# Up projection by products over both halves of the activations, high weights first, in a decoder block in fp32r parts

## What is computed

```python
up = rmsnorm(h, g_ffn[layer]) @ w_up[layer]            # 2048 -> 2 * 5632
up = causal_depthwise_conv(up, conv_w[layer], conv_b[layer])
gate, val = jnp.split(up, 2, axis=-1)
h = h + (jax.nn.silu(gate) * val) @ w_down[layer]      # 5632 -> 2048
```

## Time and profile before

| | us |
|---|---|
| median of 3 runs | 2804.72 (2804.52 to 2804.82) |
| the profiled execution | 2804.28 |
| its span, first to last instruction | 2802.8 |
| PE busy | 2797.0 (100%) |
| VectorE (DVE) busy | 2086.1 (74%) |
| ScalarE (ACT) busy | 1248.7 (45%) |

### The profile page before, as it was taken

The page is one execution under the profiler, slowest core; times in us unless marked ns, Lnnn a source line. Parts: engine busy times, 40 slices in busy tenths (PEclk is TensorE's granted clock), DMA queues, the critical chain, the costliest instruction groups (busy, mean ns, idle before and its releaser), DMA issues.

```text
span 2802.8 us, 45334 instructions
## 1 busy us (share of the span) xinstructions
PE 2797.0 (100%) x16930; PEld 2511.9 (90%) x16930; DVE 2086.1 (74%) x3913; ACT 1248.7 (45%) x1701; POOL 428.0 (15%) x579
## 2 busy tenths in 40 slices
PE   9999999999999999999999999999999999999999
PEld 7888888888889998888899999999999999999998
DVE  7776777677778777444468987888788878887884
ACT  5444343443434334333355544444444444544543
POOL 1022144323400000000000111111011101110112
PEclk9999999999999999999999999999999999999999
DMA  5464585666535555444455666666656656666667
GB/s 182 140 177 103 170 204 123 179 190 119 121 111 162 174 167 176 148 134 148 139 175 140 145 137 136 134 138 136 136 136 136 136 136 135 137 137 138 135 136 166
DMA packets 187463, 411.24 MB, mean 147 GB/s; under 512 B 22288, under 2 KB 50320, under 8 KB 186128
## 3 DMA queue, kind: packets, MB, share of 16 engines
q1 hardware_dynamic: 120240, 283.90, 33.2%
q0 software_dynamic: 67040, 124.82, 24.3%
HBM read 347.81 MB, written 112.72 MB: 164 GB/s over the span
## 4 chain that ended last, share of the span: by engine, by line
PE 97%; DVE 2%; ACT 0%; issue 0%; DMA 0%; SPq 0%; DVEq 0%; ACTq 0%
PE bank L1890 12%; PE bank L1892 12%; PE bank L1891 12%; PE bank L2160 11%; PE bank L2162 11%; PE bank L2161 11%; PE bank L2195 6%; PE bank L2196 6%; PE bank L2197 6%; PE bank L2116 3%; PE bank L2117 3%; PE bank L2118 3%; PE bank L1964 1%; PE bank L1998 1%; PE bank L2009 0%
## 5 line engine op out<-in xcount | busy, mean ns | idle before, releaser
L2160 PE MATMUL bank<-v_hi,w_hi 128*128 128x256 f32 x2464 | 697.6, 283 | 0.0
L2162 PE MATMUL bank<-v_hi,w_lo 128*128 128x256 f32 x2464 | 697.3, 283 | 0.0
L2161 PE MATMUL bank<-v_lo,w_hi 128*128 128x256 f32 x2464 | 697.3, 283 | 0.0
L937 ACT ACTIVATE w_hi<-w_raw 128x896 fp32r<-128x896 f32 (+1 forms) x528 | 445.1, 846 | 557.8 <-DVE w_raw L1686 384.5
L1693 DVE TENSOR_TENSOR w_lo<-w_raw,w_hi 128x896 fp32r<-128x896 f32 (+1 forms) x528 | 500.1, 952 | 127.0 <-ACT w_hi L937 125.9
L2160 PEld LDWEIGHTS bank<-v_hi,w_hi 128*128 128x128 f32 x2464 | 472.9, 192 | 2.0 <-issue 0.2
L2161 PEld LDWEIGHTS bank<-v_lo,w_hi 128*128 128x128 f32 x2464 | 472.9, 192 | 1.9 <-issue 0.2
L2162 PEld LDWEIGHTS bank<-v_hi,w_lo 128*128 128x128 f32 x2464 | 472.9, 192 | 0.0
L1890 PE MATMUL bank<-u_hi,w_hi 128*128 128x512 f32 x1000 | 395.4, 395 | 0.2 <-DVE w_lo L1078 0.2
L1892 PE MATMUL bank<-u_hi,w_lo 128*128 128x512 f32 x1000 | 389.9, 390 | 0.0
L1891 PE MATMUL bank<-u_lo,w_hi 128*128 128x512 f32 x1000 | 389.3, 389 | 0.0
(11 more groups left out here) (290 smaller groups left out, 4843.9 us busy)
## 6 DMA issues: line engine op xcount, KB each, us to landing
w_raw<-wslots SPq DMA_DIRECT2D x504, 256.0 KB, 2.7
w_raw<-wstream SPq DMA_DIRECT2D x189, 512.0 KB, 3.6
out_t<-stage POOLq DMA_DIRECT2D x168, 256.0 KB, 4.3
sums_scratch<-wfirst POOLq DMA_DIRECT2D x72, 448.0 KB, 5.6
g_raw<-sums_scratch SPq DMA_DIRECT2D x48, 448.0 KB, 3.3
g_raw<-wgates SPq DMA_DIRECT2D x48, 256.0 KB, 3.0
w_raw<-sums_scratch SPq DMA_DIRECT2D x24, 448.0 KB, 3.4
sums_scratch<-sums_scratch POOLq DMA_DIRECT2D x72, 128.0 KB, 4.7
```

What stands on the lines that cost most here:

```text
L937: act.activation(w4_hi[ring][:, 0:width], w4_raw[ring][:, 0:width], ACT.Copy).then_inc(w4_hi_ready, 1)
L2160: nc.tensor.matmul(out, wh, xh, start=kp == 0 and half == 0, stop=False, skip_group_check=True)
L2161: nc.tensor.matmul(out, wh, xl_, start=False, stop=False, skip_group_check=True)
L2162: ins = nc.tensor.matmul(out, wl, xh, start=False, stop=kp == KP - 1, skip_group_check=True)
```

## The change

From tile 8 on (`WIDE` = 7, 37 tiles) an up product is two matmuls in place of three. The high weights are multiplied with the high and the low activations in one matmul of 512 columns, whose moving operand is a view of two runs of 256 in `v_parts`; the low weights are multiplied with the high activations in one of 256 columns, added to the first half of the same bank. Each of the seven products has a bank of its own (0 to 6), and the two halves of a bank are added when the tile is done. In a slot the seven high matmuls come first, then, after a wait for the low weights, the seven low ones; in the tile's last slot the first three products (`EARLY`) are finished ahead of the other four. ScalarE copies the second halves of the first three banks, then of the other four (`low_halves`), and VectorE adds the first halves to them (`add_halves`), puts the sums together (`combine_wide`) and forms gate and value from them (`take_up_wide`).

The down slots of these tiles go to banks 7, 0, 1 and 7, which each wait for what was in them. A down slot's eight matmuls with high weights come ahead of its four with low weights. `take_down` moves to the head of ScalarE's position right behind the down slot; the fourth down tile's goes to position 2 of the next tile. Three semaphores of the gate stage are merged with later ones, and three new ones come in. The diff, cut to its core:

```diff
+WIDE = 7
+WIDE_PRODUCTS = [(A11, B11), (S2, T2), (S3, T3), (A22, T4), (S1, T1), (A12, B21), (S4, B22)]
+EARLY = 3
 ...
-    v_hi = [sb(f"v_hi{j}", VC, a, F32R) for j, a in enumerate(kp_at)]
-    v_lo = [sb(f"v_lo{j}", VC, a + 4 * VC, F32R) for j, a in enumerate(kp_at)]
+    v_parts = [sb(f"v_parts{j}", 2 * VC, a, F32R) for j, a in enumerate(kp_at)]
+    v_hi, v_lo = [t[:, 0:VC] for t in v_parts], [t[:, VC:2 * VC] for t in v_parts]
 ...
+    early_sum, late_sum = sb("early_sum", 4 * HALF, 28 * K), sb("late_sum", 4 * HALF, tile[10] + 64)
 ...
-    bank = [nc.alloc_psum_tensor(f"bank{j}", [P, SEQ], F32) for j in range(8)]
+    banks = nc.alloc_psum_tensor("bank", [P, 8 * SEQ], F32)
+    bank = [banks[:, j * SEQ:(j + 1) * SEQ] for j in range(8)]
 ...
+    def down_bank(d):
+        if d >= END:
+            return bank[2 + d % GROUP]
+        return bank[(7, 0, 1, 7)[d % GROUP] if wide(d // GROUP + 2) else GROUP + d % GROUP]
 ...
+            def low_halves(f, late):
+                if late:
+                    act.wait_ge(slot_done, START_F[f] + KP)
+                    act.wait_ge(s_raw_ready, f)
+                    act.activation(part_list(late_sum, 4), bank_halves(EARLY, 7, 1),
+                                   ACT.Copy).then_inc(low_copied, 1)
+                else:
+                    act.wait_ge(early_done, f - WIDE + 1)
+                    act.wait_ge(up_out, f - 1)
+                    act.activation(part_list(early_sum, EARLY), bank_halves(0, EARLY, 1),
+                                   ACT.Copy).then_inc(low_copied, 1)
 ...
-                hi_slot(n + 3)
                 f = max(g for g in range(FT) if START_F[g] <= at_)
                 q = at_ - START_F[f]
                 slots_done = place(n)[0]
+                if wide(f) and q == KP:
+                    low_halves(f, False)
+                if f >= WIDE - 1 and f < FT - 1 and q > KP:
+                    take_down(n, GROUP * (f - 2) + q - KP - 1, slots_done)
+                if n not in hi_made:
+                    hi_slot(n + 3)
 ...
-                if f > 2 and q in (2, 4):
+                if 2 < f < WIDE and q in (2, 4):
                     take_down(n, d0 - 2 + (q == 4), slots_done)
+                if f >= WIDE and q == 2:
+                    take_down(n, d0 - 1, slots_done)
 ...
-                        p1_copy(n, f)
-                    if q == KP + 1:
-                        take_down(n, d0, slots_done)
+                        if wide(f):
+                            low_halves(f, True)
+                        else:
+                            p1_copy(n, f)
                     if q == KP + 2:
                         conv_term(n, f, 0)
-                        take_down(n, d0 + 1, slots_done)
                     if q == KP + 3:
                         conv_term(n, f, 1)
                 if f == FT - 1:
                     if q == KP:
-                        p1_copy(n, f)
+                        low_halves(f, True)
+                        hi_slot(n + 4)
+                        hi_made.add(n + 1)
 ...
+            def add_halves(f, late):
+                k = 2 * (f - WIDE) + late
+                sums, j0, j1 = (late_sum, EARLY, 7) if late else (early_sum, 0, EARLY)
+                dve.wait_ge(low_copied, k + 1)
+                dve.tensor_tensor(part_list(sums, j1 - j0), bank_halves(j0, j1, 0), part_list(sums, j1 - j0),
+                                  ALU.add).then_inc(drained, 1)
+            def combine_wide(f):
+                k, done = 2 * (f - WIDE), f * DVE_STEPS4
+                dve.wait_ge(drained, k + 1)
+                dve.tensor_tensor(part(early_sum, 1), part(early_sum, 1), part(early_sum, 0),
+                                  ALU.subtract).then_inc(dve4_step, 1)
+                dve.wait_ge(dve4_step, done + 1)
+                dve.tensor_tensor(part(early_sum, 2), part(early_sum, 1), part(early_sum, 2),
+                                  ALU.subtract).then_inc(dve4_step, 1)
+                dve.wait_ge(drained, k + 2)
+                dve.scalar_tensor_tensor(out=part(early_sum, 3), in0=part(late_sum, 1), scalar=-1.0,
+                                         in1=part(early_sum, 1), op0=ALU.mult, op1=ALU.subtract).then_inc(dve4_step, 1)
+            def take_up_wide(f):
+                done = f * DVE_STEPS4
+                dve.wait_ge(dve4_step, done + 2)
+                dve.tensor_tensor(a_pad[1][:, PAD:PAD + SEQ].rearrange("p (a c) -> p a c", a=2),
+                                  part(early_sum, 2).unsqueeze(1).broadcast_to((P, 2, HALF)),
+                                  part_list(late_sum, 2), ALU.add).then_inc(dve4_step, 1)
+                dve.wait_ge(dve4_step, done + 3)
+                first_last = early_sum[:, :].rearrange("p (b c) -> p b c", c=HALF)[:, 0:4:3, :]
+                dve.tensor_tensor(a_pad[0][:, PAD:PAD + SEQ].rearrange("p (a c) -> p a c", a=2),
+                                  late_sum[:, 2 * HALF:4 * HALF].rearrange("p (a c) -> p a c", a=2),
+                                  first_last, ALU.add).then_inc(up_out, 1)
             def combine(n, f):
+                if wide(f):
+                    add_halves(f, True)
+                    combine_wide(f)
+                    return
 ...
+                if wide(f) and q == KP:
+                    add_halves(f, False)
+                sums(n + 3)
+                lo_slot(n + 2)
 ...
+            def bank_free(f, j):
+                d = GROUP * (f - 3)
+                if f == WIDE:
+                    if j >= GROUP:
+                        pe.wait_ge(down_out, GROUP + d + j - GROUP + 1)
+                    return
+                pe.wait_ge(drained, 2 * (f - WIDE) - (j < EARLY))
+                if j < 2:
+                    pe.wait_ge(down_out, GROUP + d + j + 2)
+            def wide_high(f, kp, ring, j):
+                w, x = WIDE_PRODUCTS[j]
+                both = v_parts[kp][:, :].rearrange("p (a c) -> p a c", a=2)[:, :, x * HALF:(x + 1) * HALF]
+                if kp == 0:
+                    bank_free(f, j)
+                nc.tensor.matmul(bank[j].rearrange("p (a c) -> p a c", a=2), w4_hi[ring][:, w * P:(w + 1) * P], both,
+                                 start=kp == 0, stop=False, skip_group_check=True)
+            def wide_low(kp, ring, j):
+                w, x = WIDE_PRODUCTS[j]
+                return nc.tensor.matmul(bank[j][:, 0:HALF], w4_lo[ring][:, w * P:(w + 1) * P], part(v_hi[kp], x),
+                                        start=False, stop=kp == KP - 1, skip_group_check=True)
+            def wide_products(at_, f, kp, ring):
+                for j0, j1 in ((0, EARLY), (EARLY, 7)) if kp == KP - 1 else ((0, 7),):
+                    for j in range(j0, j1):
+                        wide_high(f, kp, ring, j)
+                    if j0 == 0:
+                        pe.wait_ge(w4_ready, at_ + 1)
+                    for j in range(j0, j1):
+                        ins = wide_low(kp, ring, j)
+                    if j1 == EARLY:
+                        ins.then_inc(early_done, 1)
+                return ins
+            def down_free(d):
+                f, i = d // GROUP + 2, d % GROUP
+                if not wide(f):
+                    pe.wait_ge(down_out, d + 1)
+                elif d >= END + GROUP:
+                    pe.wait_ge(down_out, d + 1)
+                elif d >= END:
+                    pe.wait_ge(drained, 2 * (FT - WIDE))
+                elif i == 0:
+                    pe.wait_ge(down_out, GROUP + d)
+                elif i == 3:
+                    pe.wait_ge(down_out, GROUP + d - 2)
+                else:
+                    pe.wait_ge(drained, 2 * (f - WIDE) + 1)
 ...
+                if wide(f):
+                    pe.wait_ge(w4_hi_ready, at_ + 1)
+                    wide_products(at_, f, kp, ring).then_inc(slot_done, 1)
+                    return
 ...
-                pe.wait_ge(w4_ready, at_ + 1)
+                pe.wait_ge(w4_hi_ready, at_ + 1)
                 for c, d, fs, first, last in entry(n)[1]:
                     pe.wait_ge(s_ready, fs[-1] + 1)
-                    pe.wait_ge(down_out, d + 1)
+                    down_free(d)
                     if d == DOWNS[-1][0]:
+                        pe.wait_ge(w4_ready, at_ + 1)
                         ins = in_halves(ring, kk, fs, first)
                         continue
-                    out = bank[GROUP + d % GROUP][:, :]
-                    for f in fs:
-                        wh, wl = (t[ring][:, kk * P:(kk + 1) * P] for t in (w4_hi, w4_lo))
-                        sh, sl = s_hi[f % 8][:, :], s_lo[f % 8][:, :]
-                        nc.tensor.matmul(out, wh, sh, start=first and f == fs[0], stop=False)
-                        nc.tensor.matmul(out, wh, sl, start=False, stop=False)
-                        ins = nc.tensor.matmul(out, wl, sh, start=False, stop=last and f == fs[-1])
-                        kk += 1
+                    out = down_bank(d)[:, :]
```

(41 more changed lines are left out.)

14 lines of the change are left out of this document (7 added, 7 removed).

## The result

| | median us | of the kernel before, with 95% interval |
|---|---|---|
| before | 2804.77 | |
| after | 2783.60 (2783.14 to 2784.31) | 0.9924 [0.9914, 0.9935] |
| predicted | 2778.1 (2775 to 2793) | 0.9905 |

A forecast was written before the change was run, and what follows sets the result against it. The prediction took PE's own matmul stream as the bound: the profiled 2804.28 us less 27.6 for merged matmuls plus 1.0 in the tail gave 2777.7, and 0.44 for the median made 2778.1 us; range 2775 to 2793.

The forecast's parts named there:

- the bound: Whole kernel: PE's own stream of matmuls sets the time, PE being busy 100% with no wait in the changed stage.
- its own case: Whole kernel: the merge saves its full fixed parts and the loop's new work is covered; 2775 to 2782 us, chance 0.74.
- rival 1: Tile boundary: late copy, late add and `conv_term` run long, the third copy delays PE; 2782 to 2800 us, chance 0.11.
- one fixed part goes: 0.01333 us: Up slots on PE: three matmuls become two per product, saving 0.01333 us each over 2072 products, 27.6 us.
- the tail: After tile 44: the fourth down slot waits for the first copy, sharing bank 7; +1.0 us, once.
- the thinnest cover: Tile boundary: ScalarE's third copy frees bank 1 with 0.79 us to spare before the next tile's second product.
- VectorE: Loop: added work brings it to some 90% busy, 27.5 of 30.3 us per tile, but not the bound.
- its slower form: Tile boundary: reads jumping between banks go at half rate, a wait of 1.1 x 36 = 40, 2818 us; chance 0.07.
- The operand's second run: 512-column product: taken as costing 0; the rival has another 13.3 ns each, no saving on PE, 2805.7 us, chance 0.07.
- The fourth: Up slots: rival that only c of the 13.3 ns goes per product, 2778.1 + 2072 x (13.3 - c); chance 0.01.

The follow-up runs named there:

- Run 4: Changed kernel with the merged 512-column high product split again into two matmuls of 256, all else kept: 2805.96 us, ratio 1.0004.
- runs 6 and 7: Both against the changed kernel: `take_down` back behind `hi_slot` on ScalarE, 2826.15 us; the value half's `conv_term` moved ahead of the third copy, 2789.3 us.
- run 7: Changed kernel with `conv_term` of the value half moved ahead of ScalarE's third copy, behind that of the gate half: 2789.3 us.
- run 8: Changed kernel with only the fourth down tile behind tile 44 sent to bank 6 in place of bank 7: 2782.6 us.
- run 3: Changed kernel with the 512-column product streaming 512 neighbouring columns instead of two runs of 256 (other sums, same widths): 2784.1 us.

## Why the prediction was right, and where it was off

*Right:* the bound, the sign and the place. PE had no wait in the loop before and has none after; the time fell by what its stream got shorter. Run 4 shows that this comes from merging two matmuls and from nothing else in the change.

*Luck:* the prediction gave its own case 2775 to 2782 us, and 2783.6 lies above that. It lies inside the stated range because room was left there, up to 2793, for the late copy of rival 1. That loss did not come; another did, of 5.2 us, which the prediction took at nothing.

*The term that was mis-sized:* "one fixed part goes: 0.01333 us", 27.6 in all. The fixed part is right where neighbours have the same width. The prediction took the distance of a 512-column matmul from a stretch where all have 512 columns, and put it into an order where seven of them follow seven of 256. The change of width (five distances that are together 27 ns too long, and on the way back two that are together 7 ns too short) was already in the trace before: the four down slots of the earlier trace rows take 10.91 us where 48 x 0.2267 is 10.88, and the up slots behind them 20.15 where 168 x 0.1200 is 20.16. The prediction worked with the undisturbed value and passed over 0.03. It stood there once per tile. The new order has it nine times: ahead of slots 2 to 8, within the last slot and ahead of the down slots. From 30.293, by widths alone, to 30.453 is 0.160 us; the tile before lost 0.02 in this way, so 0.14 x 37 = 5.2 us of the gain went there. With 22.4 for the loop and 1.1 lost in the tail the sum is 21.3; measured were 21.2.

*The boundary:* the order of steps, their times to some hundredths and the finding that the third copy is the thinnest cover were right; runs 6 and 7 show that order on ScalarE decides there. Its 0.79 us were too much by about 0.15, since the time from a bank's release to the next matmul, 0.14 in runs 6 and 7, was left out. That did not matter in the change and did in run 7.

*The tail:* 1.0 predicted. The distance there is 1.31 us, 1.08 over the usual, and the next one 0.08; run 8 gains 1.0 by taking the wait away.

*VectorE:* 27.5 of 30.3 us predicted, 90.7%; the stretch has 90.0%. It is no bound: PE waited for it nowhere in the loop.

*Rivals:* the late copy and its slower form came only where runs 6 and 7 made the copy late; the adds and copies over three and four banks took at most 0.06 us more than the prediction had, far from the 0.8 and 1.1 of the slower form. The operand's second run costs nothing that shows (run 3). The fourth, that less than 13.3 ns goes with a product, came nearest: in effect 22.4 / 2072 = 10.8 ns went, but for the reason just told and not because the fixed part is smaller. The Trainium skill (TensorE: Matmul & The Clock Gate, "Back-to-back issue gap") has 2.5 ns for isolated matmuls; an estimate by it is 109 and 216 ns at 256 and 512 columns. These traces do not agree: behind neighbours of the same width, matmuls of 256 columns stand 120 ns apart, in run 4 too, and those of 512 columns 227.

*The rest:* in the profiled execution the up projection's first matmul starts at 1433.2 us of the span, before at 1432.1. Ahead of it only names of semaphores and of buffers were changed, and 0.9 of the lag is there within the first 16 us of the span, where the wait of 0.6 us on L2002 stands; what sets it is open. The profiled execution is the slowest of the six; the sum above is made with medians.

## What to carry to other kernels

Take the cost of an instruction from a place where its neighbours are those that it will have, and when a stretch doesn't come out at count times distance, ask where the rest is before using either number: 0.03 us once in a tile became a fifth of the gain when the change repeated it. Where matmuls of two widths must alternate, put equal widths side by side, across the borders of slots too; of the orders tried here, runs of one were the slowest. When a bank is reused across engines, write down the instruction that frees it and what stands ahead of it in its engine's order, and count the restart into the cover.

## What was not expected of the hardware

- Going from matmuls of 256 columns to 512 costs 27 ns, spread over the first five distances (233, 236, 228, 233 and 231 ns in the trace of the change, in place of 226.7), and the way back returns 7 ns (113 and 119 in place of 120). In runs of seven that is 20 ns a slot, in pairs some 47 (7 x 6.5). Why is open: no run separates the load of weights from the stream of columns, and every matmul here has its own load.
- A moving operand in two runs of 256 columns, 7 KB apart, costs nothing that shows against one run of 512 (2783.6 and 2784.1 us).
- After a wait for a ScalarE copy, PE starts 0.14 us behind the end of that copy (runs 6 and 7), and the matmul after that comes late as well: it stands 0.31 us off instead of 0.23, there and behind the wait of the tail.
